# Gathers that read the float32 rows, a fifth early expert unit, and a first group gathered pair by pair

## The chip, the cores and the metric

The kernel runs as one launch on one core of a Trainium2 chip. The metric is the device time of the launch in microseconds. Before the change three runs took 1225.74, 1225.88 and 1229.07 us; the median is 1225.88 us.

## The reference: two decoder layers with a mixture of experts

The input is x, 256 tokens of 1024 float32 values, with int32 positions and the weights of two layers. Each layer does `x = LN(alpha*x + mixer(x))` and then `x = LN(alpha*x + MoE(x))`, with alpha = 4 ** 0.25. The mixer of layer 0 is a causal convolution module beside latent attention with 8 heads, the mixer of layer 1 is attention with 16 heads and forget gates. The part that matters here is the MoE of each layer:

```python
s = sigmoid(t @ router_w)                       # 256 tokens x 64 experts
# the best 4 of 8 groups of experts by s + bias, of these the best 6 experts
w = s_of_chosen / sum(s_of_chosen) * 2.5
routed = sum over experts e of  (silu(t @ wg[e]) * (t @ wu[e])) @ wd[e] * gate[:, e]
shared = (silu(t @ sh_w_gate) * (t @ sh_w_up)) @ sh_w_down
return routed + shared
```

An expert has three matrices, gate and up (1024 x 256) and down (256 x 1024), each 1 MB in float32. All 64 experts of both layers are read, since nearly every expert has tokens.

## The kernel before

All five engines run hand-written programs that meet through semaphores: `prog_sync` issues nearly all loads on SyncE's queue, `prog_tensor`, `prog_scalar`, `prog_vector` and `prog_gpsimd` compute. A matmul here takes its weights from one operand (stationary, 128 columns at most) and streams the other. Results go to eight PSUM banks; `plan_banks` (L148) lays down in which order each bank is used, and `bank_open`, `bank_made`, `bank_read`, `bank_done` and `bank_moved` turn that order into semaphore counts.

**The ring.** Weights live in `ring`, 13 units of 1 MB. The matrix w (0 gate, 1 up, 2 down) of slot j (0 to 3) of a group of four experts has a fixed unit, so a load of the next group's matrix waits until TensorE has used the matrix that is in the unit. `refill` (L707) does so: for each piece (j, w) it waits for the bank that the last use made, then issues the load at L711. `into_place` (L714) issues without a wait of its own at L716.

**Groups.** The 64 experts of a layer are worked off in 16 groups of four. A wide group gives each expert 64 token slots and works in two pairs of experts (`gate_up`, `flip_hidden`, `down`, each with `pr` 0 or 1); a narrow group gives 32 slots and works on four at a time. `KINDS` (L53) gives the order: first (wide), single0 (narrow), back0 (narrow), turn0 (wide), back1, turn1, and so on, then a loop of narrow groups. The first group takes experts 0 to 3 and turn0 experts 4 to 7; all others come in an order sorted by the number of tokens, which the kernel computes after routing (`rank_keys`, `ranks`, on TensorE `ranked`, then `ordered`) and which SyncE reads as register values (`in_place`) before it can issue any load whose expert depends on it.

**Gathers.** Tokens are gathered to slots by matmuls: a 0/1 matrix `pick` (128 tokens x slots, for two halves tb of the tokens) is the moving operand, and 128 features of the tokens' rows are the weights. The rows are split in two float32r copies: `xs_high` is the rows rounded to float32r (ScalarE, L1674), `xs_low` what is left (VectorE, L2096). Each gather then adds both: `gather` (L1209) does four matmuls of 256 slots for a chunk c of 128 features, `pairs` (L1280) eight matmuls of 128 slots for two chunks of a narrow group. ScalarE and VectorE copy the banks to `xg` or `xn` (`gathered`, `pair`). The copies lie in `side` (high) and `V` (low), areas that the mixer has used before; the rows themselves, `xrow`, are stored so that feature chunk c is every eighth element.

**The early loads.** Ahead of a layer's MoE SyncE loads all twelve pieces of the first group, in the order `early` (L684, L690), each as soon as its unit is free (`held` names the bank to wait for), at L705. Two of them go to an area of `big` instead of the ring (`IN_YS`). The four pieces in `LEAD` (L81), for the fourth group turn0, have places of their own as well: three in `par`, which the layer norm has used, and one in `xrow` (`lead_rows`), once the copies and the accumulator have been taken from the rows. `load_lead` (L667) issues them at L669: the one for LEAD[3] ahead of the output projection's weights, LEAD[1] and LEAD[2] after the layer norm, LEAD[0] last, after the waits for `xs` and `acc_begun`. After that come the loads that need the sorted order: one at L716 once `order` is there, then at L744 the second group's gates and ups in halves, released by the semaphore `first_half` (half the chunks of a pair done) and by the bank of that pair.

**The first group on TensorE** (`wide`, L1324): eight gathers of 256 slots over the eight chunks, with `ranked` behind the fifth; `gate_up(0)`; the rest of the shared expert's up; transposes of the routing rows and of the gates; `sort`; `gate_up(1)`; then down, with the gathers for the next group between. ScalarE takes five of the eight bank copies, VectorE those of chunks 3, 5 and 7 (`DVE_FIRST`), and `ordered` runs behind VectorE's copy of chunk 5. The functions Sigmoid (routing) and Silu need different tables on ScalarE; a table load stands directly ahead of the first activation that needs it.

## Time and profile before

| what | value |
|---|---|
| median of three runs | 1225.88 us (1225.74 to 1229.07) |
| span of the profiled execution | 1227.7 us |
| its time beside the span | the page gives the span alone; it lies 1.8 us over the median |
| TensorE busy | 1061.3 us, 86% |
| VectorE, ScalarE, GpSimd busy | 415.3, 233.2, 65.9 us |
| moved by DMA | 446.73 MB, mean 364 GB/s |
| chain that ended last | TensorE 60%, DMA 28%, SyncE's queue 4%, VectorE 4% |

The profile is one execution, taken by the hardware profiler. Its page has the span in 40 slices with the busy share of each engine, of the DMA engines and the rate in GB/s. Windows give the same for a chosen stretch. The chain of waits is followed back from the last instruction: at each step to what released it. Times are microseconds from the start of the span; L1252 is line 1252 of the kernel.

### The profile page before, as it was taken

How to read it: one execution, taken by the hardware profiler on the slowest of the kernel's cores; microseconds unless marked ns; L12 is line 12 of the kernel's file. 1: busy time of each engine (PE TensorE's matmuls, PEld its weight loads, DVE VectorE, ACT ScalarE, POOL GpSimd, SP SyncE). 2: the span in 40 equal slices, each digit the busy share in tenths (PEclk: the TensorE clock that was granted, in tenths of full speed). 3: DMA queues.
4: the chain of work that ended last, by engine and by line, in shares of the span. 5: the costliest groups of instructions: out<-in, count | busy, mean ns of one | idle time of the engine just before them, and what ended most of it. 6: DMA issues, size and time to landing. Idle time of an engine off the chain costs nothing.

```text
span 1227.7 us, 19635 instructions
## 1 busy us (share of the span) xinstructions
PE 1061.3 (86%) x7794; PEld 624.9 (51%) x7794; DVE 415.3 (34%) x1023; ACT 233.2 (19%) x558; POOL 65.9 (5%) x100
## 2 busy tenths in 40 slices
PE   8999998889697997578899999988898879985775
PEld 5765664354444453344688747543444343543432
DVE  4855532223232232221345446232223232331213
ACT  2352321112121211011122224211121111110110
POOL 3141000000000000000132000000100000000000
PEclk9999999989898998789999999989899898998878
DMA  9258899999999999999991648999999999999995
GB/s 360 95 184 349 314 409 419 421 403 411 420 421 421 420 420 420 419 400 415 359 312 45 250 162 314 381 406 419 402 407 420 421 420 421 421 420 420 402 420 211
DMA packets 84829, 446.73 MB, mean 364 GB/s; under 512 B 8447, under 2 KB 26414, under 8 KB 37629
## 3 DMA queue, kind: packets, MB, share of 16 engines
q1 hardware_dynamic: 82214, 439.84, 88.7%
q0 software_dynamic: 2096, 5.47, 1.3%
q8 instruction: 68, 1.11, 0.4%
q14 instruction: 29, 0.23, 0.0%
q10 hardware_dynamic: 422, 0.08, 0.0%
HBM read 443.12 MB, written 1.05 MB: 362 GB/s over the span
## 4 chain that ended last, share of the span: by engine, by line
PE 60%; DMA 28%; SPq 4%; DVE 4%; issue 3%; ACT 1%; POOL 0%; DVEq 0%; ACTq 0%
DMA ring<-in_l_exp_w_down 15%; DMA ring<-in_l_exp_w_up 13%; PE bank L1252 12%; PE bank L1425 8%; PE bank L1463 5%; PE bank L1079 5%; PE bank L1001 4%; PE bank L1276 4%; PE bank L1288 3%; SPq L772 3%; PE bank L1082 2%; PE bank L1155 2%; PE bank L1396 2%; PE bank L1213 1%; PE bank L1381 1%
## 5 line engine op out<-in xcount | busy, mean ns | idle before, releaser
L1425 PE MATMUL bank<-ring,big 128*32 128x256 f32 x2816 | 181.2, 416 | 50.4 <-DMA ring<-in_l_exp_w_up 31.8
L1252 PE MATMUL bank<-ring,big 128*64 128x512 f32 x608 | 152.7, 635 | 43.3 <-DMA ring<-in_l_exp_w_up 43.3
L1425 PEld LDWEIGHTS bank<-ring,big 128*32 128x32 f32 x2816 | 99.6, 119 | 126.7 <-issue 64.3
L2331 DVE TENSOR_TENSOR mixT<-mixT,bank 128x512 f32<-128x512 f32 x120 | 78.5, 686 | 126.7 <-PE bank L1396 108.9
L1252 PEld LDWEIGHTS bank<-ring,big 128*64 128x64 f32 x608 | 48.4, 146 | 133.1 <-issue 132.4
L1463 PE MATMUL bank<-ring,big 128*32 128x512 f32 (+1 forms) x736 | 88.7, 623 | 20.4 <-DMA ring<-in_l_exp_w_down 17.0
L1288 PE MATMUL bank<-pick,xs_high 128*128 128x128 f32 x352 | 84.5, 282 | 0.0
L1288 PE MATMUL bank<-pick,xs_low 128*128 128x128 f32 x352 | 81.9, 275 | 0.0
L1288 PEld LDWEIGHTS bank<-pick,xs_high 128*128 128x128 f32 x352 | 67.6, 192 | 21.6 <-issue 21.6
L2301 DVE TENSOR_TENSOR big<-big,bank 128x256 f32<-128x256 f32 x22 | 9.3, 421 | 201.3 <-PE bank L1425 201.3
L1707 ACT ACTIVATE ys_high<-bank,gcol 128x512 fp32r<-128x512 f32 (+1 forms) x86 | 56.7, 677 | 95.6 <-PE bank L1276 50.9
L1288 PEld LDWEIGHTS bank<-pick,xs_low 128*128 128x128 f32 x352 | 67.5, 192 | 0.0
L1463 PEld LDWEIGHTS bank<-ring,big 128*32 128x32 f32 x736 | 25.1, 116 | 67.6 <-issue 62.1
L1276 PE MATMUL bank<-ring,big 128*64 128x512 f32 x256 | 58.5, 598 | 0.0
L1079 PE MATMUL bank<-xT,ring 128*128 128x256 f32 (+1 forms) x320 | 57.5, 339 | 0.4 <-DVE mixT L2346 0.4
L2284 DVE COPY big<-bank 128x256 f32<-128x256 f32 x44 | 18.6, 422 | 114.9 <-PE bank L1288 114.9
L1001 PE MATMUL bank<-ring,mixT 128*128 128x512 f32 x128 | 57.1, 595 | 0.0
L1396 PE MATMUL bank<-ys_high,hot 128*128 128x512 f32 x80 | 40.9, 511 | 18.7 <-issue 14.9
L1079 PEld LDWEIGHTS bank<-xT,ring 128*128 128x128 f32 x320 | 50.5, 191 | 6.5 <-issue 1.8
L2470 POOL TENSOR_TENSOR rstd<-rstd,half 128x1 f32<-128x1 f32 x10 | 10.6, 1061 | 801.3 <-DVE rstd L1814 801.3
L2248 DVE SCALAR_TENSOR_TENSOR ys_low<-bank,gcol,ys_high 128x512 fp32r<-128x512 f32 x40 | 29.9, 751 | 62.5 <-ACT ys_high L1707 62.5
L1213 PE MATMUL bank<-pick,xs_high 128*128 128x256 f32 x160 | 42.9, 304 | 0.1
(332 smaller groups left out, 1361.1 us busy)
## 6 DMA issues: line engine op xcount, KB each, us to landing
ring<-in_l_exp_w_gate SPq DMA_DIRECT2D x120, 1024.0 KB, 11.5
ring<-in_l_exp_w_up SPq DMA_DIRECT2D x120, 1024.0 KB, 16.2
ring<-in_l_exp_w_down SPq DMA_DIRECT2D x112, 1024.0 KB, 16.7
ring<-in_l_w_in SPq DMA_DIRECT2D x13, 1024.0 KB, 12.4
ring<-in_l_w_out SPq DMA_DIRECT2D x8, 1024.0 KB, 8.3
lead_par<-in_l_exp_w_down SPq DMA_DIRECT2D x6, 1024.0 KB, 12.1
ring<-in_l_exp_w_gate SPq DMA_DIRECT2D x12, 512.0 KB, 7.7
ring<-in_l_exp_w_up SPq DMA_DIRECT2D x12, 512.0 KB, 8.5
```

What stands on the lines that cost most here:

```text
L772: sp.dma_start(loop_weights(L, j, 2)[:, :, a:b], expert_weights(L, experts[j], 2)[:, :, a:b])\
L1001: ins = mm(ps[:], mixT[:, 2 * k + j, P * tb:P * tb + P], w[:, j, HALF * h:HALF * h + HALF], start=start, stop=stop)
L1079: ins = mm(ps[:, T * s + t.start:T * s + t.stop], w[:, c, P * s:P * s + P], xT[:, c, t], start=(c == 0), stop=(c == C - 1))
L1213: ins = mm(ps[:, 0:GSLOT], xs[k][:, tb, P * c:P * c + P], pick[:, tb, :], start=(tb + k == 0), stop=(tb + k == 2))
L1252: ins = mm(ps[SLOTS * q:SLOTS * q + SLOTS, :], xg[:, c, SLOTS * j:SLOTS * j + SLOTS], both[:, c, 0:n:n - 1], start=(c == 0), stop=(c == C ...
L1276: ins = mm(ps[SLOTS * q:SLOTS * q + SLOTS, :], hidT[pr][:, m, SLOTS * q:SLOTS * q + SLOTS], wt[:, m, HALF * h:HALF * h + HALF], start=(m = ...
L1288: ins = mm(ps[:, n * s:n * s + n], xs[k][:, tb, P * (2 * c + s):P * (2 * c + s) + P], pick[:, tb, 0:n], start=(tb + k == 0), stop=(tb + k ...
L1396: ins = mm(ps[:], hot[:, 0, P * tb:P * tb + P], ys[k][:, 0, HALF * h:HALF * h + HALF], start=(k == 0), stop=(k == 1))
L1425: ins = mm(ps[r, 0:HID], xn[:, c, r], loop_weights(L, j, w)[:, c, :], start=(c == 0), stop=(c == C - 1))
L1463: ins = mm(ps[r, 0:b - a], hidT[0][:, m, r], loop_weights(L, j, 2)[:, m, a:b], start=(m == 0), stop=(m == 1))
L1707: fn(ys[0][:, pr, a:b], ps[:, 0:b - a], ACT.Copy, scale=gcol[:, pr:pr + 1]).then_inc(lp.own("high"), 1)
L2331: lp.done(v.tensor_tensor(part, part, ps[:], ALU.add), (of, n))
```

## The change

The float32r copies are gone. `gather` and `pairs` read `chunk_of_rows`, the float32 rows with a step of eight elements as weights, and `pick` is float32; a chunk takes two matmuls instead of four. LEAD has a fifth piece, (0, 0), the gate of turn0's first expert. LEAD[0] lies in `side` and LEAD[4] in `V`, and both are issued between the 8th and the 9th early load, each when its area is free. `gate_up` does an expert whose gate is a lead piece in two matmuls of 256 columns per chunk. The first group gathers its first pair of experts (128 slots, two chunks to a bank, four banks), runs `gate_up(0)`, and gathers the second pair then; `ranked` stands behind the third bank, all eight banks are copied by ScalarE, and VectorE writes the order without a gather's copy ahead of it.

```diff
@@ -78,12 +78,12 @@
...
 IN_YS = [(GE - 1, 0), (GE - 1, 1)]
-LEAD = [(1, 2), (2, 2), (3, 2), (0, 2)]
+LEAD = [(1, 2), (2, 2), (3, 2), (0, 2), (0, 0)]
 LED = BEGIN["turn0"]
...
 AHEAD = 5
-RANKED_BEHIND = 4
-DVE_FIRST = (3, 5, 7)
+LEAD_BEFORE = 8
+RANKED_BEHIND = 2
@@ -202,8 +202,8 @@
...
         u.add(("pos", L), 0)
-        for c in range(C):
-            u.add(("gather", L, c), FIRST_GATHER[c])
+        for n in range(C):
+            u.add(("gather", L, n), FIRST_GATHER[n])
         wide = [("gT", 2)]
@@ -522,10 +522,10 @@
...
         acc = mixT[:, :, :].rearrange("p c t -> p (c t)").rearrange("p (a b) -> p a b", a=TB)
-        lead_rows = over("lead_rows", "xrow", 0, [P, UNIT], F32)
+        lead_side = over("lead_side", "side", 0, [P, UNIT], F32)
+        lead_v = over("lead_v", "V", 0, [P, UNIT], F32)
         lead_par = over("lead_par", "par", 0, [P, 3 * UNIT], F32)
         in_big = over("in_big", "big", 2048, [P, 2 * UNIT], F32)
-        xs = [over("xs_high", "side", 0, [P, TB, D], F32R), over("xs_low", "V", 0, [P, TB, D], F32R)]
         xg, xn = cut(big, 0, C, GSLOT), cut(big, 0, C, GE * NSLOT)
@@ -533,7 +533,7 @@
...
         hot = over("hot", "big", 7680, [P, 2, T], F32R)
-        pick = over("pick", "side", 2048, [P, TB, GSLOT], F32R)
+        pick = cut(side, 2048, TB, GSLOT)
         pickg = cut(att, 256, TB, GSLOT)
@@ -545,11 +545,8 @@
...
-        def by_piece(a, tb):
-            return a[:, tb, :].rearrange("t (c p) -> t c p", c=C)
-        def by_row(a, tb):
-            return a[:, tb, :].rearrange("t (p c) -> t c p", c=C)
+        def chunk_of_rows(tb, c):
+            return xrow[:, tb, :].rearrange("t (p c) -> t c p", c=C)[:, c, :]
@@ -603,7 +600,7 @@
...
                 n = LEAD.index((j, w))
-                a = lead_par[:, (n - 1) * UNIT:n * UNIT] if n else lead_rows
+                a = (lead_side, *(lead_par[:, k * UNIT:k * UNIT + UNIT] for k in range(3)), lead_v)[n]
             return by_chunk(a) if w < 2 else by_pair(a)
@@ -696,7 +693,18 @@
...
                     early = (11, 0, 1, 7, 8, 2, 9, 10, 3, 4, 5, 6)
-                for j, w in (divmod(k, 3) for k in early):
+                for k in early:
+                    j, w = divmod(k, 3)
+                    if k == early[LEAD_BEFORE]:
+                        if L:
+                            bank_moved(sp, ("v", 3))
+                        else:
+                            bank_read(sp, ("uT", 1))
+                        load_lead(*LEAD[0])
+                        bank_read(sp, ("ot", L, 7 if L else 3))
+                        if L == 0:
+                            sp.wait_ge(S("u_normed"), TB)
+                        load_lead(*LEAD[4])
                     if L and in_ys(0, j, w):
@@ -723,9 +731,6 @@
...
                     load_lead(j, w)
-                sp.wait_ge(S("xs"), 2 * L + 2)
-                sp.wait_ge(S("acc_begun"), TB * (L + 1))
-                load_lead(*LEAD[0])
@@ -1209,10 +1214,20 @@
...
                     for tb in range(TB):
-                        for k in range(2):
-                            ins = mm(ps[:, 0:GSLOT], xs[k][:, tb, P * c:P * c + P], pick[:, tb, :],
-                                     start=(tb + k == 0), stop=(tb + k == 2))
+                        ins = mm(ps[:, 0:GSLOT], chunk_of_rows(tb, c), pick[:, tb, :], start=(tb == 0), stop=(tb == 1))
                     return ins
+                def first_gather(n):
+                    pr, m = divmod(n, C // 2)
+                    key = ("gather", L, n)
+                    ps = bank_open(pe, key)
+                    for s in range(2):
+                        for tb in range(TB):
+                            ins = mm(ps[:, P * s:P * s + P], chunk_of_rows(tb, 2 * m + s), pick[:, tb, P * pr:P * pr + P],
+                                     start=(tb == 0), stop=(tb == 1))
+                    bank_made(ins, key)
@@ -1238,12 +1253,18 @@
...
                     for c in range(C):
-                        if lp.kind == "first" and pr == 0:
-                            bank_moved(pe, ("gather", L, c))
-                        elif lp.r is None and pr == 0:
+                        if lp.kind == "first" and c % 2 == 0:
+                            bank_moved(pe, ("gather", L, C // 2 * pr + c // 2))
+                        elif lp.kind != "first" and lp.r is None and pr == 0:
                             lp.copied_chunk(pe, LOOP_GATHER, c)
...
                             j = 2 * pr + q
+                            if in_lead(BEGIN[lp.kind] if lp.r is None else None, j, 0):
+                                for w in range(2):
+                                    ins = mm(ps[SLOTS * q:SLOTS * q + SLOTS, HID * w:HID * w + HID],
+                                             xg[:, c, SLOTS * j:SLOTS * j + SLOTS], loop_weights(L, j, w, LED)[:, c, :],
+                                             start=(c + w == 0), stop=(c + w == C))
+                                continue
                             u, n = loop_unit(L, j, 0)[0], 1 + place(j, 1)
@@ -1284,9 +1305,8 @@
...
                             for tb in range(TB):
-                                for k in range(2):
-                                    ins = mm(ps[:, n * s:n * s + n], xs[k][:, tb, P * (2 * c + s):P * (2 * c + s) + P],
-                                             pick[:, tb, 0:n], start=(tb + k == 0), stop=(tb + k == 2))
+                                ins = mm(ps[:, n * s:n * s + n], chunk_of_rows(tb, 2 * c + s), pick[:, tb, 0:n],
+                                         start=(tb == 0), stop=(tb == 1))
                         lp.made(ins, ("pair", c))
@@ -1324,11 +1344,13 @@
...
                     if lp.kind == "first":
-                        for c in range(C):
-                            bank_made(gather(c, bank_open(pe, ("gather", L, c))), ("gather", L, c))
-                            if c == RANKED_BEHIND:
+                        for n in range(C // 2):
+                            first_gather(n)
+                            if n == RANKED_BEHIND:
                                 ranked(lp)
                         gate_up(lp, 0)
+                        for n in range(C // 2, C):
+                            first_gather(n)
                         shared_gate_up(0, 1, 1, AHEAD)
@@ -1494,7 +1516,6 @@
...
-                pe.wait_ge(S("xs"), 2 * L + 2)
                 pe.wait_ge(S(f"moe{L}_pick"), 1)
@@ -1669,12 +1690,10 @@
...
                     xt(1 + 2 * L, k)
-                for tb in range(TB):
-                    act.wait_ge(S("ln_done"), 4 * L + tb + 1)
-                    fn(by_piece(xs[0], tb), by_row(xrow, tb), ACT.Copy).then_inc(S("xs_high"), 1)
                 xt(1 + 2 * L, 2)
...
                 bank_done(fn(sco, ps[:, 0:TB * NE].rearrange("p (a e) -> p a e", a=TB), ACT.Sigmoid), ("router", L))
+                act.wait_ge(S("ln_done"), 4 * L + TB)
                 for tb in range(TB):
@@ -1770,9 +1789,15 @@
...
-                for c in range(C):
-                    if c not in DVE_FIRST:
-                        gathered(bank_read, bank_done, ("gather", L, c))
+                def first_gathered(n):
+                    pr, m = divmod(n, C // 2)
+                    ps = bank_read(act, ("gather", L, n))
+                    bank_done(fn(xg[:, 2 * m:2 * m + 2, P * pr:P * pr + P], ps[:, 0:2 * P].rearrange("p (c s) -> p c s", c=2),
+                                 ACT.Copy), ("gather", L, n))
+                for n in range(C):
+                    first_gathered(n)
                 alone_groups(L, wide, narrow)
@@ -2089,12 +2114,7 @@
...
-                for tb in range(TB):
-                    if tb:
-                        xt(1 + 2 * L, (3,))
-                    dve.wait_ge(S("xs_high"), 2 * L + tb + 1)
-                    v.tensor_tensor(by_piece(xs[1], tb), by_row(xrow, tb), by_piece(xs[0], tb), ALU.subtract)\
-                     .then_inc(S("xs"), 1)
+                xt(1 + 2 * L, (3,))
@@ -2371,19 +2391,16 @@
...
-                def first_gathered():
+                def rank_and_gates():
...
                     ranks()
-                    for c in DVE_FIRST:
-                        gathered(bank_read, bank_done, ("gather", L, c))
-                        if c == RANKED_BEHIND + 1:
-                            ordered(first)
+                    ordered(first)
                     gate_values()
...
                 first = ExpertLoop(L, "first", banks, S, bank, i=0)
-                select(first, "wide", 0, 1, first_gathered)
+                select(first, "wide", 0, 1, rank_and_gates)
                 dve.wait_ge(S("acc_begun"), TB * (L + 1))
```

## Rows read from the trace of the kernel before

**Rows 1.** Windows in layer 0: window, length, busy us by engine, clock, DMA share, GB/s

```profile
116.00:118.00 2.00, 2.00 (x9) 1.10 (x8) 1.26 (x3) 0.00 (x0) 0.00 (x0) 1.00 0.00 0
138.00:142.00 4.00, 4.00 (x24) 1.84 (x24) 2.68 (x12) 1.67 (x2) 0.00 (x0) 1.00 0.36 96
172.00:592.00 420.00, 345.72 (x2812) 185.45 (x2810) 107.72 (x200) 60.31 (x148) 3.56 (x4) 0.92 1.01 415
```

**Rows 2.** Windows in layer 1, same columns

```profile
724.00:736.00 12.00, 12.00 (x45) 5.77 (x42) 5.39 (x9) 1.64 (x4) 1.56 (x1) 1.00 0.02 9
756.00:760.00 4.00, 4.00 (x30) 2.76 (x31) 2.38 (x9) 2.21 (x4) 0.00 (x0) 1.00 0.04 12
800.00:1200.00 400.00, 331.11 (x2610) 175.73 (x2609) 104.55 (x194) 58.38 (x144) 3.54 (x4) 0.90 1.01 415
```

**Rows 3.** The page: its span, and one kind of DMA issue with its size

```profile
span 1227.7 us, 19635 instructions
...
ring<-in_l_exp_w_up SPq DMA_DIRECT2D x120, 1024.0 KB, 16.2
```

**Rows 4.** Timeline of SyncE's queue in layer 0: start, duration, instruction

```profile
117.66 0.33 SPq L705 DMA_DIRECT2D ring<-in_l_exp_w_up  x1
...
139.49 0.36 SPq L716 DMA_DIRECT2D ring<-in_l_exp_w_gate  x1
```

**Rows 5.** Chain of waits around the first group, layer 0: start, duration, what

```profile
127.50 5.41 PE bank L1155 x48
...
134.28 2.62 PE bank L1213 x20
136.90 0.20 PE bank L1296 x2
137.10 0.11 PE bank L1297 x2
137.21 1.63 PE bank L1213 x12
138.84 7.02 PE bank L1252 x32
...
147.47 0.71 PE bank L1305 x4
...
155.63 0.84 PE bank L1288 x8
```

**Rows 6.** Single issues at 139.5, 160.1, 779.9, 237.6, 254.0 us: issue to landing

```profile
DMA to landing us min/median/max: 4.9/4.9/4.9
...
DMA to landing us min/median/max: 6.9/6.9/6.9
...
DMA to landing us min/median/max: 5.8/5.8/5.8
...
DMA to landing us min/median/max: 8.1/8.1/8.1
...
DMA to landing us min/median/max: 6.7/6.7/6.7
```

**Rows 7.** Chain of waits: a projection of layer 1, and a transpose of xrow

```profile
675.83 7.10 PE bank L1079 x32
...
123.10 0.87 PE bank L819 x8
```

**Rows 8.** Timeline of VectorE: the permutation and the order

```profile
135.30 0.52 DVE L2199 TENSOR_SCALAR att<-iota,att 64x64 f32<-64x64 f32 x2
...
138.26 0.20 DVE L2205 CAST order<-bank 1x64 int32<-1x64 f32 x1
```

**Rows 9.** Timeline of ScalarE: copies of gathers, and table loads

```profile
135.03 1.34 ACT L1690 ACTIVATE big<-bank 128x256 f32<-128x256 f32 x3 [5.33 <-PE bank L1213]
...
138.80 1.28 ACT L1684 ACT_TABLE_LOAD   x1
...
62.38 1.28 ACT L1553 ACT_TABLE_LOAD   x1
63.68 0.40 ACT L1553 ACTIVATE att<-att,mx 128x128 f32<-128x128 f32 x1
```

**Rows 10.** Window behind the loop of narrow groups, layer 0, columns of rows 1

```profile
510.00:516.00 6.00, 0.08 (x1) 0.00 (x0) 0.69 (x1) 0.00 (x0) 0.00 (x0) 0.50 1.01 418
```

## The prediction

> **What bounds the kernel now.** I read the slices first, then windows, then the queue of issues, then the chain of waits. In each layer there is one long stretch, 172 to 592 us and 800 to 1200 us, in which the DMA engines are busy throughout (share 1.01, 415 GB/s) [rows 1, 2]. A unit, one third of an expert, is 1024 KB [rows 3], so it costs 1.05 MB / 0.415 to 0.42 MB per us = 2.5 us there. In these stretches TensorE is busy 346 of 420 us and 331 of 400 us: work taken from it buys nothing by itself. The layer ends when its last unit has landed and been used, so the question for every edit is by how much the byte stream gets ahead.
>
> Ahead of both long stretches the stream has holes. Layer 0: nothing moves in 116 to 118 us, and 138 to 142 us runs at 96 GB/s [rows 1]. The first hole ends with the issue at 117.66 us, which had waited for the output projection; the second with the one at 139.49 us, the first load whose address depends on the sorted order of experts [rows 4]. Layer 1 has the same two: 9 GB/s over 724 to 736 us and 12 GB/s over 756 to 760 us [rows 2]. Bytes put into these holes, or a second hole that ends sooner, are the whole gain on offer. Between the second hole and the long stretch TensorE is on the path: gather, gate and up of pair 0, shared expert, sort, gate and up of pair 1, pair gathers, down [rows 5], and each of its releases frees ring units for loading.
>
> **One more early unit.** Five units instead of four are loaded ahead for the group turn0, and the one that sat in xrow moves to `side`. It and the new one, in V, go out between the 8th and 9th early load. In layer 0 `side` is free after the last transpose of u, V earlier, so both can be issued near 102 us. They need 5.0 us, while the engines stand still from about 116 us until 117.66 plus what a lone load spends before its bytes move: 4.9 us to landing [rows 6] less 2.5 = 2.4, so until 120.1. About 4 us of the 5.0 go into the hole and 1 us pushes the loads behind, which nobody awaits before 138 us; it is absorbed ahead of the second hole. In layer 1 the hole of 12 us takes both whole. The load of rows, which ran just ahead of the second hole, is gone from there. The new unit no longer has to be loaded in the long stretch: 2.5 us a layer. It can be lost only where TensorE frees the ring too late. At turn0, gate and up of pair 1 free the ring at 237.6 us, and the first load then lands after 8.1 us; the next such place, at 254.0 us, has 6.7 [rows 6]. Against 4.9 for a lone load the slack is 3.2 and 1.8 us, and TensorE has waited for turn0's weights before both, so it comes earlier with them. Expert 0 of turn0 now needs two matmuls of 256 columns per chunk where one of 512 stood. The two column groups work side by side (32 in 7.02 us, 0.44 a pair [rows 5]), so the cost lies between 0 and, if nothing overlapped, 8 x 0.44 = 3.5 us. I take 0, the order of issue keeping both halves fed; the upper end would eat the slack and cost at most 0.5 us a layer.
>
> **No float32r copies.** Four passes over the rows on ScalarE and VectorE go in each layer, and a load no longer waits for them. What hides them now is the router: its matmuls run back to back behind the transposes and end just ahead of 127.50 us [rows 5], and the chain comes to that point over TensorE alone, touching no copy. Worth 0; below nothing is excluded, since only waits go.
>
> **The gathers.** A float32r gather of 256 columns is issued each (2.62+1.63)/32 = 0.13 us [rows 5]. Float32 matmuls of 128 columns come at 5.41/48 = 0.113 us [rows 5], of 256 columns at 7.10/32 = 0.22 us [rows 7]. So the first group's gather stays 32 instructions, 3.7 instead of 4.25 us, but only half is ahead of pair 0. The picks let it start at 134.28 us [rows 5] in both. Twelve matmuls take 1.4 us to 135.7; the permutation that ranking needs is there at 135.30 + 0.52 = 135.82 [rows 8], so ranking waits 0.2 us, takes 0.31 [rows 5] and ends at 136.2. VectorE has nothing in between now and writes the order at 136.3 instead of 138.26 [rows 8]: 2.0 us sooner, and the issue at 139.49 goes with it, 1 us of queue work behind. Four matmuls later, at 136.7 instead of 138.84, gate and up of pair 0 begin: 2.1 us sooner, and with them the ring's releases at their half and end. ScalarE's four copies, 1.34/3 = 0.45 us each [rows 9], keep ahead of the chunks. **The stream restarts 2.0 us earlier.**
>
> It does not keep all of it. Gate and up of pair 0 end at 143.7, pair 1's 16 gathers at 145.6, the shared expert's rest at 146.4. But the sigmoid and silu tables differ. Before, the table load of 1.28 us ran at 138.80 [rows 9], idle time, because it directly follows the last copy of a gather in ScalarE's order. Now that copy is pair 1's, ending near 146.0. The load ends at 147.3, silu and the copy of routed rows at 148.0, and the sort starts at 148.05 instead of 147.47 [rows 5]: gate and up of pair 1 come 0.6 us later than before. (Cover gone: that is the price.) The Trainium skill, "ScalarE: Activation LUTs", section "What ACT_TABLE_LOAD costs", charges a drain of 1.38 us besides each load; in this trace the load at 62.38 ends at 63.66 and the activation starts at 63.68 [rows 9], so no drain shows. By that rule the sort would be 2.0 us late and the total 4.6 us instead of the 7.4 below.
>
> Behind that, a pair of chunks is gathered by 4 matmuls instead of 8 (0.84 us [rows 5]), 0.4 us less; beside the wait for the transposed hidden rows about 0.35 of it counts. So the release of pair 0's down weights is 0.6 - 0.35 = 0.25 us later than before, the next 0.1 earlier, the narrow group's gates 0.9 earlier. The loads issued on these are where the stream could run dry. Before they landed after 6.9 us in layer 0 and 5.8 in layer 1 [rows 6]: slack over 4.9 of 2.0 and 0.9. The stream can be ahead by at most 2.0 - 0.25 = 1.7 and 0.9 - 0.25 = 0.7 us (rounded). Those are the terms. Bounds: 0 if ScalarE is later still, 2.0 if it is not late. Elsewhere the halved gathers lie in DMA's shade: 0.
>
> **Sum.** Layer 0: 2.5 + 1.7 = 4.2. Layer 1: 2.5 + 0.7 = 3.2. Together 7.4 us: the profiled span 1227.7 [rows 3] becomes 1220.3. The page gives no other time of that execution; its span lies 1.8 us over the median of the three timed runs, 1225.88. The same 7.4 off that gives 1218.5.
>
> **Rivals.**
> *Only the units count* (1220.9, chance 0.14): the restart's gain is eaten by late releases, 2 x 2.5. For it: slack of 0.9 in layer 1. Against it: 2.0 in layer 0.
> *A table load holds ScalarE 1.4 us longer than its row* (1221.3, chance 0.03): the sort 2.0 us late, 4.6 us in all. Against: the start at 63.68 [rows 9].
> *Nothing is late* (1216.9, chance 0.16): 2 x (2.5 + 2.0). For it: the slack is read to a tenth, and the least time of a load is taken from one row.
> *The extra unit doesn't carry* (1223.5, chance 0.09): the split gate and slow ring releases at turn0 give the 2.5 back, only 1.7 + 0.7 stay. Against: 3.2 us of slack there [rows 6].
> *Strided weights are slow* (1226, chance 0.05): the gathers now load their weights from xrow with a step of eight elements, where the copies lay packed. If each took 0.23 us, pair 1's gather would end 3.8 us and the sort some 4 us late, making the stream dry by 2 to 3 us a layer, which eats the 5.0. Against: the transposes at 123.10 load the same strided rows and come at 0.87/8 = 0.109 us [rows 7], packed float32 at 0.113 [rows 5]. The Trainium skill, "SBUF — State Buffer", section "Door 1: The DMA port swizzle", says each access to a new 16-byte line pays, four float32 at the most being free; here every element is on a new line and the row shows no price.
> *The clock falls* (slower, 1236, chance 0.07): with half of the pair gathers gone TensorE idles more. The granted clock is 0.92 and 0.90 over the long stretches [rows 1, 2], and 0.50, its lower level of 1.2 GHz, in 510 to 516 us, where it is idle [rows 10]. The 420 us hold 14 groups of 12 units, 30 us each; their matmuls take 346 x 0.92 / 14 = 23 us at the full level, 45 at the lower, less 4 for the halved gathers at that level. A group that runs wholly at the lower level is so 41 against 30 us; the queue's slack takes 2 of the 11. One in each layer costs 2 x 9 = 18, less 7.4: 10 us slower, and it decides from the first such group, 9 against 7.4. Against: the saving is under 2 us of 30 in a group, and the work behind a late landing, which is what idles the engine, stays as it is.
>
> **Numbers.** Forecast 0.46. Alone its range is 1216.5 to 1220.5. Faster or slower means over 0.3%, 3.7 us, about what this kernel's measurement tells from no change. Faster: 0.46 + 0.16 + 0.14 + 0.03, less 0.03 for those that measure short of it, 0.76. Same: 0.09 + 0.05 and those, less what of the strided case is slower, 0.16. Slower: 0.08. The range is 1214 to 1224.5: it holds the first rivals and most of the fourth.
>
> **What would show it.** The order written about 2.0 us after the picks' end instead of 4.1; table load behind pair 1's last copy and the sort 0.6 us late; no gap at 116 to 118 us, a shorter one at 724 to 736; first landings at the down weights near 4.9 us; seven ring loads for turn0 beside five lead loads; the last expert unit of layer 0 landing 4.2 us earlier. I am wrong if the gathers' spacing exceeds 0.12 us, if gate and up of turn0's pair 0 take more than 9 us, or if the long stretch shows under 415 GB/s.

## The result, and the profile after

| | median us | runs | ratio to before |
|---|---|---|---|
| before | 1225.88 | 5 (1224.87 to 1229.07) | |
| after | 1265.07 | 5 (1264.36 to 1269.09) | 1.0318, 95% interval 1.0299 to 1.0338 |

The change made the kernel 39 us slower; 1218.5 had been forecast, with 1214 to 1224.5 as its range. In the profiled executions the span went from 1227.7 [rows 3] to 1267.1 us, TensorE's busy time from 1061.3 to 1180.8 us and the mean of a weight load of the pair gathers from 192 to 333 ns. First the chain of waits of the changed kernel around the first group of layer 0 (start, duration, what), to be laid beside [rows 5]; `x24` and the like count records, that is, matmuls as the profile lists them:

```profile
131.61 5.96 PE bank L1228 x24
...
137.87 2.10 PE bank L1228 x8
...
146.99 7.83 PE bank L1228 x32
...
154.84 0.38 ACT big L1796
...
155.25 1.28 ACT L1703
...
157.25 0.71 PE bank L1325 x4
...
165.41 1.89 PE bank L1308 x8
...
188.41 12.45 DMA ring<-in_l_exp_w_down
```

L1228 is the first gather, pair by pair. Before pair 0 it makes 24 + 8 = 32 records and not the 16 that were forecast, and each takes 0.25 us, not 0.11. The same again stands behind pair 0. The pair gathers at L1308 have 8 records as before and take 1.89 us where they took 0.84 [rows 5]. From the first gather to the wait for the down weights at 188.41 us pass 56.8 us; in the kernel before 40.2, from 134.28 [rows 5] to 174.43. The difference of 16.6 adds up: 8.06 - 4.25 = 3.8 ahead of pair 0, 7.8 behind it, 3 x 1.05 + 1.06 = 4.2 in four pair gathers, 1.7 for the last copy and the table load, less 0.9 of shared expert that left the chain.

The page gives the pair gathers' records over both layers, L1288 in the kernel before and L1308 in the changed one (shapes, number | busy us, mean ns | idle before):

```profile
L1288 PE MATMUL bank<-pick,xs_high 128*128 128x128 f32 x352 | 84.5, 282 | 0.0
L1288 PE MATMUL bank<-pick,xs_low 128*128 128x128 f32 x352 | 81.9, 275 | 0.0
```

```profile
L1308 PE MATMUL bank<-side,xrow 128*128 128x128 f32 x704 | 180.7, 405 | 0.0
```

Then windows (window, length, busy us of PE, PEld, DVE, ACT, POOL, clock, DMA share, GB/s), first where the first hole was, then behind the second, then the long stretch, and last what is left of layer 1's first hole:

```profile
116.00:118.00 2.00, 1.36 (x12) 1.39 (x13) 1.93 (x4) 0.55 (x2) 1.06 (x1) 1.00 0.89 295
...
160.00:180.00 20.00, 20.00 (x91) 11.24 (x87) 3.08 (x10) 3.86 (x10) 0.00 (x0) 1.00 0.69 232
...
172.00:592.00 420.00, 391.00 (x2772) 242.34 (x2775) 110.11 (x203) 60.60 (x150) 4.21 (x4) 0.96 0.98 404
...
750.00:754.00 4.00, 4.00 (x10) 1.71 (x9) 3.13 (x7) 0.00 (x0) 1.56 (x1) 1.00 0.00 0
```

The first hole of layer 0 is filled: 295 GB/s where nothing moved [rows 1]. (This execution is 2.7 us ahead there; from 106 to 120 us no other 2 us of it have less than 401 GB/s.) That of layer 1, 12 us long before [rows 2], is shorter: nothing moves from 750 to 756 us. Behind the second hole of layer 0 a new one opens, 232 GB/s over 160 to 180 us, where the kernel before moved 404: the loads there are issued on TensorE's releases of the ring, and these come late. And the long stretch falls to 404 GB/s with TensorE busy 391 of 420 us, 45 more than before [rows 1]. What that looks like in the chain, later in layer 0 and at the start of layer 1's group:

```profile
222.76 4.11 PE bank L1217 x16
...
264.04 4.01 PE bank L1308 x16
...
333.44 17.66 DMA ring<-in_l_exp_w_up
...
761.70 1.16 PE bank L824 x8
...
829.94 12.52 DMA ring<-in_l_exp_w_down
```

Between 201.10 and 333.01 us the chain names no DMA at all. The kernel before waits for the down weights from 174.43 us and then, in that stretch, three times more for weights:

```profile
174.43 12.65 DMA ring<-in_l_exp_w_down
...
207.01 11.39 DMA ring<-in_l_exp_w_up
...
239.96 18.26 DMA ring<-in_l_exp_w_up
...
295.23 14.93 DMA ring<-in_l_exp_w_up
...
794.23 12.49 DMA ring<-in_l_exp_w_down
```

The transposes of layer 1 start at 761.70 where they started at 742.60, 19.1 late, and the chain reaches its down weights at 829.94 against 794.23, 35.7 late.

### The profile page after: what moved, and what is told of

Read it like the earlier page. It is cut to its first block, busy times and chain, and to the rows that moved or that the text cites. A ratio compares the mean times of both kernels' runs of the same rounds, so it can differ in the third digit from the quotient of the medians.

```text
span 1267.1 us, 19820 instructions
## 1 busy us (share of the span) xinstructions
PE 1180.8 (93%) x7890; PEld 763.1 (60%) x7890; DVE 405.5 (32%) x1013; ACT 226.8 (18%) x560; POOL 67.2 (5%) x100
## 3 DMA queue, kind: packets, MB, share of 16 engines
HBM read 443.12 MB, written 1.05 MB: 351 GB/s over the span
## 4 chain that ended last, share of the span: by engine, by line
PE 75%; DMA 14%; DVE 4%; SPq 3%; issue 3%; ACT 1%; POOL 0%; DVEq 0%; ACTq 0%
PE bank L1308 11%; PE bank L1273 11%; PE bank L1447 9%; DMA ring<-in_l_exp_w_down 8%; PE bank L1297 6%; DMA ring<-in_l_exp_w_up 6%; PE bank L1485 5%; PE bank L1084 4%; PE bank L1006 4%; PE bank L1418 3%; SPq L777 3%; PE bank L1217 3%; PE bank L1228 3%; PE bank L1087 2%; PE bank L1160 2%
## 5 line engine op out<-in xcount | busy, mean ns | idle before, releaser
L1308 PEld LDWEIGHTS bank<-side,xrow 128*128 128x128 f32 x704 | 172.4, 333 | 21.5 <-issue 21.5
L1308 PE MATMUL bank<-side,xrow 128*128 128x128 f32 x704 | 180.7, 405 | 0.0
L1447 PE MATMUL bank<-ring,big 128*32 128x256 f32 x2816 | 167.4, 395 | 14.2 <-ACT big L1741 12.0
L1273 PE MATMUL bank<-ring,big 128*64 128x512 f32 x576 | 145.2, 608 | 10.5 <-DMA ring<-in_l_exp_w_up 10.5
L1447 PEld LDWEIGHTS bank<-ring,big 128*32 128x32 f32 x2816 | 91.9, 114 | 85.2 <-ACT big L1741 18.0
L1273 PEld LDWEIGHTS bank<-ring,big 128*64 128x64 f32 x576 | 44.8, 139 | 87.1 <-issue 86.6
L1485 PE MATMUL bank<-ring,big 128*32 128x512 f32 (+1 forms) x736 | 80.9, 577 | 7.8 <-DMA ring<-in_l_exp_w_down 4.2
L1217 PEld LDWEIGHTS bank<-side,xrow 128*128 128x128 f32 x256 | 62.4, 334 | 7.5 <-issue 7.5
L1217 PE MATMUL bank<-side,xrow 128*128 128x256 f32 x256 | 66.9, 413 | 0.0
L1418 PE MATMUL bank<-ys_high,hot 128*128 128x512 f32 x80 | 44.4, 555 | 18.0 <-issue 14.7
L1297 PE MATMUL bank<-ring,big 128*64 128x512 f32 x256 | 58.5, 598 | 0.0
L1485 PEld LDWEIGHTS bank<-ring,big 128*32 128x32 f32 x736 | 22.4, 109 | 51.2 <-issue 46.3
L1418 PEld LDWEIGHTS bank<-ys_high,hot 128*128 128x128 f32 x80 | 17.4, 218 | 45.8 <-issue 22.3
## 6 DMA issues: line engine op xcount, KB each, us to landing
ring<-in_l_exp_w_up SPq DMA_DIRECT2D x120, 1024.0 KB, 15.8
```

The lines of the kernel that those rows point to most:

```text
L1217: ins = mm(ps[:, 0:GSLOT], chunk_of_rows(tb, c), pick[:, tb, :], start=(tb == 0), stop=(tb == 1))
L1273: ins = mm(ps[SLOTS * q:SLOTS * q + SLOTS, :], xg[:, c, SLOTS * j:SLOTS * j + SLOTS], both[:, c, 0:n:n - 1], start=(c == 0), stop=(c == C ...
L1297: ins = mm(ps[SLOTS * q:SLOTS * q + SLOTS, :], hidT[pr][:, m, SLOTS * q:SLOTS * q + SLOTS], wt[:, m, HALF * h:HALF * h + HALF], start=(m = ...
L1308: ins = mm(ps[:, n * s:n * s + n], chunk_of_rows(tb, 2 * c + s), pick[:, tb, 0:n], start=(tb == 0), stop=(tb == 1))
L1418: ins = mm(ps[:], hot[:, 0, P * tb:P * tb + P], ys[k][:, 0, HALF * h:HALF * h + HALF], start=(k == 0), stop=(k == 1))
L1447: ins = mm(ps[r, 0:HID], xn[:, c, r], loop_weights(L, j, w)[:, c, :], start=(c == 0), stop=(c == C - 1))
```

## The experiments

Thirteen kernels were run. In the diffs the surroundings are left out, and `...` stands for more; ratios are to runs of the kernel before on the same chip.

**The gather's weights packed (a_packed).** The changed kernel; its LayerNorm writes the rows in chunk order, so that the gathers' weights lie side by side; the transposes of the rows and ScalarE's copy to the accumulator read them in the new order. Everything else stays.

```
-            return xrow[:, tb, :].rearrange("t (p c) -> t c p", c=C)[:, c, :]
+            return xrow[:, tb, P * c:P * c + P]
-                    layer_norm(tb, xrow[:, tb, :], 2, 3)
+                    ...  # the last step: read by (p c), written by (c p)
```

> The changed kernel, with one thing different: the layer norm ahead of the experts writes the rows chunk by chunk, so that the gathers' weights lie packed instead of with a step of eight elements. Theory 1 (the step makes each weight load slow): a gather record falls from 0.25 us to 0.113 at 128 columns and 0.22 at 256, a pair of chunks from 2.06 to 0.9 us, and the time from 1265 to 1222 to 1228 us. Rival (float32 gathers are slow for themselves, as each is issued as two records, and the step is innocent): spacing stays near 0.25 us and the time at 1260 to 1267 us.

1239.8 us (1237.3 to 1243.8), ratio 1.0098 (1.0070 to 1.0126): 27 of the 39 us are gone, not all of them as expected (1222 to 1228). The chain of this kernel, layer 0:

```profile
134.34 2.93 PE bank L1228 x24
...
145.69 3.78 PE bank L1228 x32
...
149.89 1.28 ACT L1704
...
151.90 0.71 PE bank L1325 x4
...
160.06 0.89 PE bank L1308 x8
```

0.12 us a record instead of 0.25. The number of records has stayed.

**The step alone, in float32r (b_strided).** The kernel before, with its copies left in row order and read with a step of eight.

```
-    xs[k][:, tb, P * c:P * c + P]
+    by_row(xs[k], tb)[:, c, :]
-    fn(by_piece(xs[0], tb), by_row(xrow, tb), ACT.Copy)
+    fn(xs[0][:, tb, :], xrow[:, tb, :], ACT.Copy)
```

> The kernel before with only the layout of the float32r copies changed: they are written in the order of the rows and the gathers read them with a step of eight. Count of matmuls, type and everything else stay. Theory 1: each record of a gather goes from 0.11 to 0.2 us or more, a narrow group gets 3 to 4 us longer on TensorE, and the time passes 1240 us. Rival (a step costs only in float32): 0.11 us a record and 1223 to 1228 us, the copies being cheaper if anything.

1279.1 us (1277.5 to 1280.9), ratio 1.0416 (1.0398 to 1.0434). So the step costs whatever the type. Here it costs 51 us and in the changed kernel 27, since the two types don't lose the same: a float32r record of 256 columns goes from 0.13 to 0.25 us, a packed fp32 one takes 0.23 already (b_f32, below) and goes to 0.26 (L1217, 4.11 us for 16). The gathers' busy time on TensorE rose by 171 us in this kernel and, from a_packed to the change, by 112. Its chain has the first gather as 20 records in 5.07 us and 12 in 3.08, against 2.62 and 1.63 [rows 5], and pairs in 1.85:

```profile
134.18 5.07 PE bank L1213 x20
...
139.56 3.08 PE bank L1213 x12
...
159.44 1.85 PE bank L1288 x8
```

**The disputed cost by itself (micro_step).** A kernel of its own in which TensorE issues blocks of 32 matmuls with nothing to wait for; it computes none of the reference and was run once.

> A kernel of its own: after 42 matmuls to warm up, 16 blocks of 32 matmuls each back to back from SBUF tiles that nothing else uses: float32 weights with a step of 1, 2, 4, 8 elements against 128 packed columns; steps 1 and 8 against 256, 8 against 512; 64 weight columns with step 8; packed weights against a moving operand with step 8; transposes of packed and of step 8; float32r weights with steps 1, 2, 8 at 128 columns and 1, 8 at 256. Theory 1: float32 is two records each, step 1 takes 0.11 us a record, step 8 0.24 at 128 columns, the moving step costs nothing, float32r shows the same dependence, a transpose at step 8 stays at 0.11 because it loads once where float32 loads more than once. Rival (something in the kernel, a port shared with another engine or tile): step 8 takes 0.11 us here as well.

Its groups by line (operation, shapes, number of records | busy us, mean ns | idle before). `rows` is the operand with the step, but in L92, where `other` is:

```profile
L76 PE MATMUL bank<-other,rows 128*128 128x128 f32 x64 | 7.3, 275 | 0.0
L78 PE MATMUL bank<-other,rows 128*128 128x128 f32 x64 | 7.7, 281 | 0.0
L80 PE MATMUL bank<-other,rows 128*128 128x128 f32 x64 | 15.1, 397 | 0.0
L82 PE MATMUL bank<-other,rows 128*128 128x128 f32 x64 | 15.4, 401 | 0.0
L84 PE MATMUL bank<-other,rows 128*128 128x256 f32 x64 | 14.0, 379 | 0.0
L86 PE MATMUL bank<-other,rows 128*128 128x256 f32 x64 | 15.5, 403 | 0.0
L88 PE MATMUL bank<-other,rows 128*128 128x512 f32 x64 | 27.7, 592 | 0.0
L90 PE MATMUL bank<-other,rows 128*64 128x128 f32 x64 | 7.9, 285 | 0.0
L92 PE MATMUL bank<-other,rows 128*128 128x128 f32 x64 | 15.2, 413 | 0.0
L96 PE MATMUL bank<-ident,rows 128*128 128x128 f32 x32 | 3.7, 275 | 0.0
L98 PE MATMUL bank<-picks,rounded 128*128 128x128 f32 x32 | 3.8, 276 | 0.0
L102 PE MATMUL bank<-picks,rounded 128*128 128x128 f32 x32 | 7.9, 435 | 0.0
L104 PE MATMUL bank<-picks,rounded 128*128 128x256 f32 x32 | 6.0, 369 | 0.0
L106 PE MATMUL bank<-picks,rounded 128*128 128x256 f32 x32 | 7.9, 405 | 0.0
```

Each line is 32 matmuls. fp32 (L76 to L92) has 64 records, so one product is two records; float32r (L98 to L106) and transposes (L96) have 32. Busy time over records gives the spacing. fp32 weights of 128 columns: step 1 0.11 us (L76), step 2 0.12 (L78), step 4 0.24 (L80), step 8 0.24 (L82). A wider moving side hides the step: at 256 columns 0.22 packed and 0.24 with step 8 (L84, L86), at 512 0.43 with step 8 (L88), twice the packed 0.22 of half the width (L84). With 64 weight columns at step 8 a record takes 0.12, half as long (L90); 64 packed columns were not run, so how much of it the step costs is not shown. Packed weights and a moving operand with step 8 (L92) cost the same 0.24, where no price had been expected. float32r: 0.12 packed, 0.25 with step 8 (L98, L102), at 256 columns 0.19 and 0.25. A transpose of rows with step 8 takes 0.12 (L96): it shows no step, and [rows 7] was a transpose. The row doesn't tell which of its two operands is the weights, but in a product both pay (L82, L92). Packed float32r at 256 columns takes 0.19 here and 0.13 in the kernel before [rows 5]; why is not known.

**The first gather pair by pair (b_pairwise).** The kernel before with this order alone, float32r and packed as it was, all eight copies on ScalarE.

```
-                        for c in range(C):
-                            bank_made(gather(c, ...), ("gather", L, c))
+                        for n in range(C // 2):
+                            first_gather(n)
...
                         gate_up(lp, 0)
+                        for n in range(C // 2, C):
+                            first_gather(n)
```

> The kernel before with only the first group gathered pair by pair, in float32r from packed copies, all eight banks copied by ScalarE. 64 records of 128 columns instead of 32 of 256: 7.2 instead of 4.3 us, half of it ahead of the first gate and up. The first gate and up starts 0.3 us earlier, the second 3.3 us (rest of the gather) plus the table load's 1.3 us later, less what the earlier start gives: 3 to 4.5 us later. With a slack of 2.0 and 0.9 us in the two layers the time rises by 3 to 6 us, to 1229 to 1232 us. Rival (the pair order gains 2 us a layer as forecast): 1221 to 1223 us.

1233.9 us (1231.0 to 1234.8), ratio 1.0046 (1.0032 to 1.0060): slower by itself. The chain shows why:

```profile
134.01 2.87 PE bank L1223 x24
...
137.18 1.04 PE bank L1223 x8
138.22 7.02 PE bank L1262 x32
145.24 3.73 PE bank L1223 x32
...
149.39 1.28 ACT L1696
...
151.40 0.71 PE bank L1315 x4
```

Gathering 2 x 128 columns costs 3.9 + 3.7 = 7.6 us where 256 at once cost 4.25 [rows 5]; pair 0 starts only 0.6 us sooner, and the sort at 151.40 is 3.9 late, 1.3 of it ScalarE's table.

**Undoing it in the packed version (a_packed_whole).** The first group gathered whole again, eight chunks of 256 columns, with chunks 3, 5 and 7 copied by VectorE.

> The packed version of the changed kernel with the first group gathered whole, eight chunks of 256 columns ahead of gate_up, as before; only the order and width of the first gather differ from the packed version. Theory pair by pair: 24 + 8 + 32 records of 128 columns at about 0.12 us and a second load of the same weights come to more than the kernel before spent, and the gathers for pair 1 delay the pair behind it; before with the pairwise gather alone came out 1233.9 against 1227.7. Undone, the packed version gains 4 to 6: 1234 to 1236 (the clock's fall in layer 1, if it is there again, included). Rival, the unit: the gap between packed and before lies in the stride-free copies and the LayerNorm, then 1239 to 1241.

1234.1 us (1229.1 to 1236.9), ratio 1.0050 (1.0027 to 1.0073). It gives back what pair by pair had cost.

**The table load (a_packed_warm).** A tiny Silu activate behind the fourth copy: `fn(warmed[:], ident[:, 0:1], ACT.Silu)`.

> The packed version with one tiny Silu activate behind the fourth copy of the first gather, so that ScalarE's table is loaded (1.28 us) while TensorE is in gate_up of pair 0 and not between the last copy and the sort. Theory: the sort waited 1.07 us for that load in before with the pairwise gather, so each layer gains about 1.0: 1238 (1236.5 to 1239). Rival: something else is as late (pair 1's weights or the copy of chunk 7), then 1239 to 1241.

1237.7 us (1235.2 to 1239.3), ratio 1.0073 (1.0050 to 1.0096), beside 1.0098: the direction is right, the intervals overlap. In its chain the sort is 1.4 us behind the end of pair 1's gather, 151.22 against 149.80, instead of 2.4 (151.90 against 149.47). The mechanism is shown, its 2 us in the median are not.

**The fifth early unit (a_packed_4lead, a_whole_fill1_4lead).** `LEAD` loses `(0, 0)` and SyncE its load.

> The packed version without the fifth early unit of each layer (its load goes back to its place in the stream). Theory unit: 1 MB taken in the idle stretch of the DMA engines is worth 2.5 us a layer at 415 GB/s: 1245 (1243 to 1246). Rival, TensorE: behind the hole TensorE with its longer gathers is the bound of the stretch and gives the lead back: 1239 to 1241.

1241.4 us (1236.4 to 1241.9), ratio 1.0093 (1.0059 to 1.0126), beside 1.0098 with the unit: no gain shows, as the rival has it, but by the intervals one of 3 us is not excluded.

> The same without the fifth early unit of each layer. In the pairwise packed version the unit was worth nothing that shows (1241.4 without, 1239.8 with, ranges overlapping; from the 100th megabyte of layer 0 on it was even 1 us earlier without). Theory TensorE: that was since the longer gathers, not the stream, bound the stretch behind the hole; with the whole gather the stream is the bound again and the unit carries its 2.5 a layer: 5 more than the version with it. Rival: the unit is worth nothing here either, within 1.5 of it.

1238.2 us (1233.4 to 1239.3), ratio 1.0080 (1.0054 to 1.0107), beside 1.0058 with it: 3 us, of 5 forecast, again with intervals that overlap.

**TensorE's clock in layer 1 (a_packed_fill, a_whole_fill1).** In all packed versions the second block's LayerNorm is longer (its last step takes 2.06 instead of 1.28 us a block; it reads two operands with a step of eight), TensorE stands still in the meantime, 1.65 us in a_packed_whole, and the profile then shows the lower clock. The filling turns the first block's rows over again in that pause, 20 blocks in both layers or 14 in layer 1 alone.

```
+                    if n % 2 and tb and g == 0:
+                        for k in range(FILL):
+                            flip(ps[...], xrow[:, 0, ...], ident[:])
+                        pe.wait_ge(S("ln_done"), 2 * (n - 1) + tb + 1)
```

> The packed version of the changed kernel, in which TensorE also turns 20 blocks of the first token block's rows over again while the second block's LayerNorm ends (their result is overwritten by the real transposes). Theory clock: in the packed version's layer 1 TensorE was busy 2.01 of 4 us in 746:750, and its granted clock fell to 0.52 and 0.50 in 750:754 and 754:758, so that the router's 32 matmuls took 6.26 us where the kernel before has 3.52, and the 48 of L1160 7.92 where it has 5.41: about 5 us lost. With the work in the pause the clock stays at 1.00 there, the first gather of layer 1 starts near 760 instead of 764.7, and the median falls by about 5, to 1235 (1232 to 1237). Rival, the LayerNorm: the packed version is late in layer 1 because its LayerNorm writes rows in chunk order (2.06 us instead of 1.28 each); then the filling changes nothing (1239 to 1241), or the extra work delays the real transposes by what remains of it.

1238.3 us (1235.6 to 1240.2), ratio 1.0079 (1.0048 to 1.0110), not the 1235 expected.

> Packed rows, first group gathered whole, five early units a layer, and in layer 1 alone 14 blocks turned over again in TensorE's pause before the second block's rows. Theory clock: the version without these 14 lost 5 in layer 1 to the granted clock of 0.50 (L1160 x48 7.86 instead of 5.41, L1193 x32 5.96 instead of 3.52) and came out 1234.1; with the clock held it is 1229 (1226.5 to 1231), level with before. Rival, LayerNorm: the time is in the 2 x 0.8 us by which it is longer, then 1233 to 1235.

1234.5 us (1231.8 to 1237.6), ratio 1.0058 (1.0038 to 1.0078), where the version without it has 1.0050. Windows of layer 1 (columns as above), first a_packed_whole, then a_whole_fill1:

```profile
741.00:744.00 3.00, 1.35 (x13) 1.16 (x12) 2.10 (x2) 0.00 (x0) 0.45 (x1) 1.00 1.03 429
744.00:748.00 4.00, 4.00 (x29) 4.00 (x26) 0.69 (x1) 1.88 (x2) 0.00 (x0) 0.69 1.01 426
748.00:752.00 4.00, 4.00 (x20) 4.00 (x20) 0.86 (x12) 1.24 (x2) 0.00 (x0) 0.50 1.01 426
```

```profile
748.00:752.00 4.00, 3.81 (x35) 3.57 (x34) 1.65 (x2) 1.88 (x2) 0.00 (x0) 1.00 1.00 420
752.00:756.00 4.00, 4.00 (x38) 4.00 (x38) 1.88 (x23) 2.33 (x3) 0.00 (x0) 1.00 1.01 428
```

Without the filling TensorE is busy 1.35 of 3 us, then its clock goes to 0.50 (1.2 GHz), and the same 48 records of the shared expert take 7.86 us; with it the clock stays at 1.00 and they take 5.41. From the transposes to the first gather that is 16.3 against 11.4 us (743.67 to 759.92, 749.01 to 760.38). So the fall and its price of 5 us are shown in these executions. But the medians don't move by 5. One reason is seen: the filled execution was 5.3 us later at its transposes, and it was so already at VectorE's last sum ahead of the first block's LayerNorm (736.37 against 731.11 us), before the filling, where the two programs are the same. Whether the fall comes in the timed executions too stays open; the mean clock of a whole execution is 0.955 in both profiled ones and doesn't tell.

**The order one chunk earlier (b_order).** The kernel before, `RANKED_BEHIND` 3 for 4, and DVE's ordering one copy earlier.

> The kernel before, in which the ranking matmuls and DVE's ordering come one chunk of the first gather earlier. Theory, TensorE bound: gate_up of pair 0 ends the wait and not the ranking, so nothing moves (-0.5 to +0.5). Rival, ordering bound: the sort's copies are late, then each layer gains up to 0.6 and the median falls by 1.

1227.5 us (1226.5 to 1231.3), ratio 1.0009 (0.9996 to 1.0021). In its profile the order is written 2.5 us behind the begin of the first gather (134.38 and 131.85) instead of 4.0 (138.26 [rows 8] and 134.28 [rows 5]), so the edit did its work. The order's time, on which the forecast spent most of its working, is not the bound.

**The float type alone, and the unit on top (b_f32, b_f32_5lead).** The kernel before with one packed fp32 copy in place of the float32r pair, then with (0, 0) in V as well.

```
-                        for k in range(2):
-                            ins = mm(ps[:, 0:GSLOT], xs[k][:, tb, P * c:P * c + P], pick[:, tb, :],
...
+                        ins = mm(ps[:, 0:GSLOT], xs[:, tb, P * c:P * c + P], pick[:, tb, :], ...
```

> The kernel before with its rows copied once into chunk order as plain fp32 (ScalarE's copy as before, DVE's subtraction gone) and gathered by one fp32 product in place of the float32r pair: packed weights, LayerNorm, early units and whole first gather as before. It prices the float type by itself. Theory width: a record of 256 columns took 0.131 us in float32r (L1213 x32 4.25) and 0.230 in fp32 (L1217 12 and 20 records in 2.84 and 4.51), one of 128 columns 0.105 and 0.111; so the first gather is 3.1 longer in each layer on the path that ends the hole, the other wide gathers are partly behind the stream: 1232.5 (1230 to 1235). Rival, the LayerNorm: the packed version with whole gather is 1234.1 because its LayerNorm delays TensorE by 1.6 a layer and its clock falls; then this one is 1226 to 1229.

1235.0 us (1233.2 to 1237.2), ratio 1.0065 (1.0045 to 1.0085). The chain of b_f32:

```profile
133.75 4.56 PE bank L1212 x20
...
138.62 2.79 PE bank L1212 x12
```

32 records as before, but 7.35 us instead of 4.25 [rows 5]: at 256 columns fp32 takes 0.23 us a record, float32r 0.13. A pair at 128 columns takes 0.89 us as in a_packed, against 0.84.

> The same with the unit (0,0) as a fifth early one, in V, loaded where the changed kernel loads it. Theory unit: with and without it the packed kernel with the whole gather came out 1234.5 and 1238.2, so about 3.7 less than b_f32, and if b_f32 is at the low end this is the fastest of all, near 1224. Rival: TensorE bounds the stretch behind the hole and the unit brings less than 1.

1232.0 us (1228.7 to 1237.8), ratio 1.0035 (1.0020 to 1.0051): 3 us less, with intervals that overlap a little. None of the kernels beats the one before.

**The sum.** Along one line of kernels, each ratio turned into us over before: b_f32 +8, with the fifth unit +4, with the LayerNorm in chunk order in place of the copy (a_packed_whole) +6, pair by pair (a_packed) +12, with the step of eight (the change) +39. So: float type 8, unit -4, LayerNorm (with the clock behind it, and the unit that moved from `xrow` to `side`) 2, pair by pair 6, step 27. By the intervals each of these is uncertain by 3 to 4.5 us, so of the small ones only the sign is well told, of the LayerNorm's not even that. They are prices along this line; in another order they can differ, as the step's 51 us in b_strided show, while pair by pair costs 6 in both places (b_pairwise).

## Why the prediction was wrong

- **The step that failed first:** "So the first group's gather stays 32 instructions, 3.7 instead of 4.25 us, but only half is ahead of pair 0", and with it "a pair of chunks is gathered by 4 matmuls instead of 8". I took the chain's counts for matmuls. An fp32 product leaves two records, so the 0.113 us of L1155 was half a matmul. One fp32 product does replace two float32r ones, and the number of records stays: L1288 had 352 + 352 in both layers, L1308 has 704, and the first gather went from 32 to 64. The 0.84 us of a pair was never to be halved; packed, it became 0.89 (a_packed, b_f32).
- **The step that cost most:** the rival of strided weights had the right price per record, 0.23 us, but 0.05 for its chance and 2 to 3 us a layer for its effect. Its chance came from [rows 7]: the transposes load the same rows at 0.109 us. They read the same rows, and the micro kernel shows the same price (L96), but a transpose is no product: L82 has 0.24. The row was of another operation. Its effect was charged to the first group's gather alone, 3.8 us for 32 records; with twice the records it is in every gather, 15.8 of the 16.6 us in layer 0 up to 188 us together with the count, and then in all groups. In time the step was 27 of the 39 us. The rule that was set aside, from the Trainium skill, "SBUF — State Buffer", section "Door 1: The DMA port swizzle", says that a line of 16 bytes needs two accesses to run at full rate: step 2 in fp32 has two and costs 5% (L78), step 4 has one and doubles the record (L80). The same note calls four float32 free, which the prediction repeated; L80 contradicts it. With a price at every new line and the right count the forecast would have pointed to slower; by how much the rule doesn't say.
- **"Elsewhere the halved gathers lie in DMA's shade: 0"** failed for the same reason. The shade was 420 - 346 = 74 us in layer 0 [rows 1]; 45 of it were used up on average, and group by group more than there was, where the chain ran over TensorE from 201 to 333 us. An engine that is busy 82% of a stretch has no shade of 18% at every place.
- **The terms for the order** were of no use. The order came at 137.91 us with a gather begun at 131.61, 6.3 behind it, not 2.0 sooner than 4.0 but 2.3 later; and b_order shows that 1.5 us of it move nothing. (That gather began 2.7 us sooner than the 134.28 of before. b_order, the same program as the kernel before up to there, began it at 131.85, so 2.4 us come without any edit.)
- **The early unit, 2.5 a layer:** its mechanism was right. Both loads went out at 99.56 and 99.98 us in layer 0, the hole was filled, and the split gate cost nothing (L1264 and L1273 alternate at 0.22 us, 32 in 7.0). Its size was about 3 us for both layers where the stream is the bound (b_f32 and a_whole_fill1 with and without it), where 5 had been forecast, and nothing that shows where TensorE is (a_packed_4lead). In layer 1 the two loads went out at 737.40 and 745.86 us.
- **The table load behind pair 1's last copy** came as worked out, 155.25 us with the sort at 157.25, and no drain behind it: 156.53 to 156.54. It was 0.4 us more than its 1.28 for the copy ahead, and small beside the rest.
- **The clock** did not fall for lack of work in the change; its mean over 172 to 592 us rose to 0.96 from 0.92 [rows 1]. Only packed versions show a new fall, ahead of the first group of layer 1, a place that the rival did not name.

## What to carry to other kernels

Before a copy goes, ask what it did besides its name: here the float32r copies also put the rows in an order in which TensorE can read them at full rate, and made wide gathers of 256 columns cheaper than plain fp32. Count records per operation on a line whose matmuls are known before a duration is carried to another type, and take no price for a product from a transpose. A gain from an earlier start is worth only what the same edit leaves of it on the engine that frees the buffers.

## What the runs showed of the hardware

- An fp32 matmul is two records of 0.11 us at 128 columns and 0.22 at 256; a float32r one is one of 0.12 (0.13 to 0.19 at 256), micro_step and [rows 5]. The Trainium skill, "FP8 and Floating Point Precision", section "TensorE Precision Notes", counts four passes for true FP32. The trace shows two records, each about as long as twice its columns at 2.4 GHz: 0.22 us against 0.213 at 256 (L84), 0.43 against 0.427 at 512 (L88), which fits two passes a record. At 128 columns the one record of float32r takes as long (L98), so the length of a record there doesn't tell the passes.
- At 128 columns a step of 8 float32 doubles the record, in fp32 for the weights (0.24 us against 0.11) and for the moving operand (0.24), in float32r for the weights (0.25 against 0.12); a step of 4, run for fp32 weights, does the same (0.24). At 512 columns it is hidden (0.43). A step of 2 in fp32 costs 5%, and a transpose pays nothing (0.12).
- In layer 1 of all four packed versions without filling TensorE stood still for 1.65 to 1.99 us ahead of the second block's transposes, and its granted clock then fell to 0.50 (1.2 GHz) for some 10 us; in none of the three with filling did it. In b_f32 the same pause is 0.81 us, and the clock stayed at 1.00.
